# The recurrence's conv of block B ahead of the norm's scaling, that of C among the first four output blocks

## The chip, the cores and the metric

One Trainium2 chip, one core. The metric is the device time of one execution in microseconds (us), as the median of several runs.

## What is computed

One inference step of a small hybrid decoder: one Mamba-2 layer (SSD, a recurrence over chunks of tokens), then one multi-head latent attention layer with a paged cache, for 8 sample sequences of 4 new tokens, 16 meta tokens and a prompt of 256, in all TOK = 304 columns. The change touches the Mamba layer alone:

```python
h = rmsnorm(x, norm_g)
proj = h @ w_in                                  # z | x, B, C | dt
xbc, conv_new = causal_conv(xbc, conv_prev, ...) # 4 taps, bias, then silu
...                                              # the recurrence gives y
y = y * silu(z)
yg = y.reshape(bt, L, 8, 512)                    # 8 groups
yg = yg * rsqrt(mean(yg * yg) + EPS)             # the norm, group by group
return x + (yg * gate_norm) @ w_out
```

The channels fall into 8 groups. A group has four blocks of 128 channels of z, four of x, one of B and one of C; B and C are the fifth and sixth block that the convolution runs over (`xB = 4`, `xC = 5`).

## The kernel before

All work is written out by hand for five engines, with semaphores between them. TensorE multiplies in float32r in three products for every pair (`mm3`, L110 to L112: high by high, low by high, high by low). Weights come in units of 1 MB: SP loads `raw` (L588), ACT makes the high part `w_hi` (`split`, L935, two halves), POOL subtracts it to make the low part `w_lo` (L720, two halves); two buffers of each.

The loop runs over g, the groups. In a turn g:

- TensorE makes the ten input blocks of group g (`in_block`, k = 0 to 9: z 0 to 3, then x 0 to 3, B at k = 8, C at k = 9), with steps of the recurrence of group g - 1 between them (`heads(g - 1, k)`); the last, at k = 8, is the sum of squares of y, `squares`.
- Then it makes the sixteen output blocks of group g - 1 (`out_block`, c = 0 to 15, 12 products each), with steps that prepare group g between them (`start(g, c)`: at c = 6 x is turned, at c = 9 B and C are used). An output block needs `y_lo` (c = 0: half one for its first six products, half two for the rest), its weights, and a free bank: it waits until DVE's work on the block two before is done.

DVE goes through the same order. `evac` takes an input block out of its bank (L1096, L1097) into `cbuf[k % 2]` one iteration later than TensorE made it; `add_out` (L1101) adds an output block to x. `conv(g, k)` runs the taps of a block: tap 0 is L1115, taps 1 to 3 are L1117 on the same accumulator `cacc`, then two small copies keep the last columns (L1122, L1123) and raise `conv_saved`. Each tap waits for the one before (`v`). Tap 0 waits for the evacuation and for `old_done`, which ACT raises when it has put the old columns in front (`conv_past`, L943). The blocks x 0 to 3 have their conv at k = 5 to 8. B's four taps stand at c = 0 to 3, one behind each `add_out`, and C's at c = 4 to 7.

At k = 9 DVE evacuates B, then runs `heads(g - 1, 9)`: `scaled` (L1227, four instructions, y times the norm's factor and gain; waits for `y_rstd`) and `y_low` (L1233, two halves, waits for ACT's `y_hi`, L1006). ACT at k = 9: a split, `conv_past` of B, then `root` (L999, L1001: `y_rstd`) and `y_hi` twice. After that it has, for c < 16, four rounds n: a split, then n = 0: silu of z and `conv_silu` of x 0 to 3; n = 1: `conv_silu` of B and C (L956, L958), which waits for C's conv; n = 2 and 3: `e_cum` and `decay`. SP at n = 1 stores `conv_new` once it is saved and loads `s_t` after `xc_done`.

In turn 0 there is no group before: the input blocks come in another order and no output block is made.

Of the kernel before, what the change touches and what calls it, by code (L numbers as in the profile page):

```python
# [515 lines left out]
def mamba_stage(nc, m, psum, d, stores):  # L516
# [36 lines left out]
    xB, xC = 4, 5  # L553
# [17 lines left out]
    def block_wait(eng, kind, g, k):  # L571
        eng.wait_ge(blk_done, at[kind, g, k] + 1)

    def in_wait(eng, kind, g, k):
        eng.wait_ge(in_out, in_at[kind, g, k] + 1)

    with nc.Block() as block:
# [505 lines left out]
        def _(dve):  # L1083
            v = Serial(dve, dve_step)

            def evac(kind, g, k):
                block_wait(dve, kind, g, k)
                src, rs = DENSE[at[kind, g, k] % 2], m["rs"]
                if kind == "z":
                    if k == 0:  # L1090
                        y_gated.wait(dve, g - 2, PAIRS - 1)
                    nc.vector.tensor_tensor(gate[g % 2][:, k, :], src[:, 0:TOK], rs[:], ALU.mult).then_inc(in_out, 1)
                else:
                    conv_saved.wait(dve, g if k >= 2 else g - 1, k - 2 if k >= 2 else CONV_BLK - 2 + k)
                    buf = cbuf[k % 2]
                    nc.vector.tensor_tensor(by_seq(buf, 7)[:, :, 3:7], by_seq(src, 4), by_seq(rs, 4), ALU.mult)  # L1096
                    nc.vector.tensor_tensor(buf[:, 59:CB], src[:, N_SAMPLE:TOK], rs[:, N_SAMPLE:TOK], ALU.mult).then_inc(in_out, 1)  # L1097
# [5 lines left out]
            def conv(g, k, taps=range(4)):  # L1103
                buf, acc = cbuf[k % 2], cacc[:, k, :]
                cw = lambda t: m["conv_w"][:, g, k, t:t + 1]
                new = conv_new[g % 2]
                for t in taps:
                    if t == 0:
                        in_wait(dve, "c", g, k)
                        old_done.wait(dve, g, k)  # L1110
                        if k == 0:
                            ys_done.wait(dve, g - 1, 1)
                            if g >= 2:
                                dve.wait_ge(conv_stored[g % 2], 16 * (g // 2))
                        v(nc.vector.tensor_scalar(acc, buf[:, 0:CO], cw(0), m["conv_b"][:, g, k:k + 1], ALU.mult, ALU.add))  # L1115
                        continue
                    ins = nc.vector.scalar_tensor_tensor(acc, buf[:, t:t + CO], cw(t), acc, op0=ALU.mult, op1=ALU.add)  # L1117
                    if t < 3:
                        v(ins)
                        continue  # L1120
                    ins.then_inc(conv_done.sem, 1)
                    nc.vector.tensor_copy(new[:, k, 0:DEC_BATCH, :], by_seq(buf, 7)[:, :, 4:7])  # L1122
                    nc.vector.tensor_copy(new[:, k, DEC_BATCH, :], buf[:, CB - 3:CB]).then_inc(conv_saved.sem, 1)  # L1123
# [5 lines left out]
            def x_back(g, n):  # L1129
                t = TILE_ORDER[n]  # L1130
                rows, h = TILE_N[t], slice(g * HPG, (g + 1) * HPG)
                xn_done.wait(dve, g, n)
                y_done.wait(dve, g - 1, PAIRS - 1)
                sp_done.wait(dve, g - 1, 0)
                if g == 0 and n == 0:
                    dve.wait_ge(steps.stored, 16)
                times(m["xdt"][0:rows, t, :], XN[n][0:rows, :], m["dt_n"][0:rows, t, h])
                times(m["xwp"][0:rows, t, :], XN[n][0:rows, :], m["wp_n"][0:rows, t, h]).then_inc(xn_out.sem, 1)

            def samples_back(g):  # L1140
                xn_done.wait(dve, g, 3)
                up_done.wait(dve, g - 1, 3)
                times(m["xws"][:, :], CBA[:, REP], m["ws_q"][:, g, :], 2).then_inc(xn_out.sem, 1)

            def b_back(g):
                bn_done.wait(dve, g, 0)
                nc.vector.tensor_copy(m["b_n"][0:48, 0, :], BN[0:48, 0:STATE]).then_inc(bn_out.sem, 1)
                nc.vector.tensor_copy(m["b_n"][:, 1:3, :], BN[:, STATE:3 * STATE].rearrange("p (t n) -> p t n", t=2)).then_inc(bn_out.sem, 1)

            def b_spread(g):  # L1150
                wide = [P, DEC_BATCH, STATE]
                nc.vector.tensor_tensor(m["b_diag"][:], BN[:, 3 * STATE:4 * STATE].rearrange("p (a n) -> p a n", a=1).to_broadcast(wide),
                                        m["diag"][:].rearrange("p (b a) -> p b a", a=1).to_broadcast(wide), ALU.mult).then_inc(bd_done.sem, 1)

            def c_spread(g):
                xc_done.wait(dve, g, 1)
                nc.vector.tensor_copy(m["c_diag"][:, :, 0:DEC_SEQ], xc[:, xC, 0:N_SAMPLE].rearrange("p (b t) -> p b t", t=DEC_SEQ)).then_inc(cd_done.sem, 1)

            def cb_back(g):
                cb_done.wait(dve, g, 0)  # L1160
                nc.vector.tensor_tensor(m["cb"][0:48, 0:304], CBA[0:48, 0:304], m["mask"][0:48, 0:304], ALU.mult).then_inc(cb_out.sem, 1)
                cb_done.wait(dve, g, 1)
                nc.vector.tensor_tensor(m["cb"][:, 304:688], CBB[:, 0:384], m["mask"][:, 304:688], ALU.mult).then_inc(cb_out.sem, 1)

            def skip(g, p):
                ins = nc.vector.tensor_scalar(y[:, p, :], xc[:, p, :], m["d_skip"][:, g, p:p + 1], None, ALU.mult)
                if p == PAIRS - 1:
                    ins.then_inc(y_set.sem, 1)

            def mix(g, e):  # L1170
                dec_done.wait(dve, g, e)
                cb_out.wait(dve, g, 1)
                dc = dec_at(g, e)
                if g == LAST and e >= 2:
                    nc.vector.tensor_tensor(dc[0:48, 0:304], dc[0:48, 0:304], m["cb"][0:48, 0:304], ALU.mult)
                    nc.vector.tensor_tensor(dc[:, 304:688], dc[:, 304:688], m["cb"][:, 304:688], ALU.mult).then_inc(mix_done.sem, 1)
                else:
                    nc.vector.tensor_tensor(dc[:], dc[:], m["cb"][:], ALU.mult).then_inc(mix_done.sem, 1)
# [88 lines left out]

            def start(g, c):
                if c < 4:
                    conv(g, xB, (c,))  # L1270
                elif c < 8:
                    conv(g, xC, (c - 4,))
                elif c < 11:
                    if c == 8:
                        samples_back(g)
                    x_back(g, c - 8)
                if c == 9:
                    c_spread(g)
                if c == 11:
                    cb_back(g)  # L1280
                if c == 12:
                    b_back(g)
                if c == 13:
                    b_spread(g)
                if c == 14:
                    skip(g, 0)
                    skip(g, 1)
                if c == 15:
                    skip(g, 2)
                    skip(g, 3)  # L1290
                if g == LAST and c >= 14:
                    mix(g, c - 14)
# [31 lines left out]
            for g in range(GROUPS):  # L1324
                of_g = blocks[at["z" if g else "c", g, 0]:][0:IN_UNITS]
                if g == 0:
                    evac(*of_g[0])
                    conv(0, 0)
                    evac(*of_g[1])
                    conv(0, 1)  # L1330
                    steps.rooted(dve)
                    steps.sums(dve)
                    evac(*of_g[2])
                    conv(0, 2)
                    evac(*of_g[3])
                    steps.turned_back(dve)
                    conv(0, 3)
                    evac(*of_g[4])
                for k in range(IN_UNITS if g else 0):
                    if k:  # L1340
                        evac(*of_g[k - 1])
                    elif g == 1:
                        evac("z", 0, PAIRS - 1)
                    heads(g - 1, k)
                    if 5 <= k < 9:
                        conv(g, k - 5)
                for c in range(KT):
                    if g == 0 and c % 4 == 0:
                        evac(*of_g[CONV_BLK - 1 + c // 4])
                    if g and c == 0:  # L1350
                        evac(*of_g[IN_UNITS - 1])
                    if g:
                        add_out(g - 1, c)
                    start(g, c)
# [1743 lines left out]
```

## Time and profile before

| | us |
|---|---|
| median of 3 runs | 2270.61 (2270.43 to 2272.24) |
| the profiled execution | 2272.74 |
| its span, first to last instruction | 2271.0 |
| PE busy | 2172.0 (96% of the span) |
| DVE busy | 1423.9 (63%) |
| ACT busy | 1081.5 (48%) |
| POOL busy | 1063.0 (47%) |

The Mamba layer fills roughly the first 950 us. Times in the trace are counted from the span's start. Busy PE is time in which a matmul is in the array; matmuls overlap, so the distance from one start to the next is what they cost. A time in brackets behind an instruction is the idle time of its engine before it, with what ended it.

### The profile page before, as it was taken

To read this page: it belongs to the slowest core of one execution; us is meant where nothing else is said; L and a number is where in the kernel's file an instruction comes from. 1 tells how busy PE (TensorE), PEld (TensorE's weight loads), DVE (VectorE), ACT (ScalarE), POOL (GpSimd) and SP (SyncE) were. 2 spreads that over 40 slices of the span, in tenths; PEclk is the share of its full clock that TensorE was granted. 3 is DMA by queue.
4 is the path that set the end of the run, shared out by engine and by line. 5 is a ranking of instruction groups with operands and counts; after the bars stand their busy time and mean duration, and the time that the engine had idled before them with its cause. 6 is when DMAs were issued, how large, how long until landed. Compare 5 with 4: busy or idle time off the path is not lost. (4 is left out here: it accounts for less than half of the span.)

```text
span 2271.0 us, 37449 instructions
## 1 busy us (share of the span) xinstructions
PE 2172.0 (96%) x13816; PEld 1864.2 (82%) x13816; DVE 1423.9 (63%) x2329; ACT 1081.5 (48%) x2696; POOL 1063.0 (47%) x694
## 2 busy tenths in 40 slices
PE   7999999999999999799998995999999999999799
PEld 7989988899988899598997763787787877877599
DVE  7877777778786868654214667566565665665510
ACT  5454444444444444554344554554554544545332
POOL 2655656565656565266772004533333333333166
PEclk9999999999999999899999996999999999999899
DMA  5664646464656565334443312202122122021544
GB/s 179 228 222 162 225 175 223 152 226 167 219 173 211 182 218 204 126 114 146 166 167 124 132 69 86 74 22 74 31 64 64 32 64 74 22 74 33 226 159 145
DMA packets 80768, 309.69 MB, mean 136 GB/s; under 512 B 14626, under 2 KB 22178, under 8 KB 55250
## 3 DMA queue, kind: packets, MB, share of 16 engines
q1 hardware_dynamic: 80594, 307.41, 39.5%
q8 instruction: 105, 1.72, 0.3%
q14 instruction: 69, 0.57, 0.1%
HBM read 279.72 MB, written 27.66 MB: 135 GB/s over the span
## 5 line engine op out<-in xcount | busy, mean ns | idle before, releaser
L720 POOL TENSOR_TENSOR w_lo<-raw,w_hi 128x1024 fp32r<-128x1024 f32 x216 | 539.4, 2520 | 396.3 <-ACT w_hi L935 396.3
L110 PE MATMUL bank<-h_hi,w_hi 128*128 128x304 f32 (+1 forms) x1520 | 470.2, 309 | 14.4 <-DVE w_lo L339 10.5
L112 PE MATMUL bank<-h_hi,w_lo 128*128 128x304 f32 (+1 forms) x1520 | 458.3, 302 | 0.0
L111 PE MATMUL bank<-h_lo,w_hi 128*128 128x304 f32 (+1 forms) x1520 | 456.5, 300 | 0.0
L935 ACT ACTIVATE w_hi<-raw 128x1024 fp32r<-128x1024 f32 x216 | 216.6, 1050 | 340.2 <-PE bank L112 333.7
L110 PE MATMUL bank<-b_hi,a_hi 128*128 128x512 f32 x896 | 357.6, 399 | 16.1 <-POOL a_lo L2503 8.4
L111 PE MATMUL bank<-b_lo,a_hi 128*128 128x512 f32 x896 | 350.9, 392 | 0.0
L112 PE MATMUL bank<-b_hi,a_lo 128*128 128x512 f32 x896 | 350.5, 391 | 0.0
L110 PEld LDWEIGHTS bank<-h_hi,w_hi 128*128 128x128 f32 x1520 | 286.4, 188 | 26.2 <-DVE w_lo L339 10.5
L111 PEld LDWEIGHTS bank<-h_lo,w_hi 128*128 128x128 f32 x1520 | 286.9, 189 | 2.3 <-issue 1.7
L112 PEld LDWEIGHTS bank<-h_hi,w_lo 128*128 128x128 f32 x1520 | 286.4, 188 | 0.0
L2554 ACT ACTIVATE two<-two 128x128 f32<-128x128 f32 x512 | 152.2, 299 | 146.5 <-DVE two L2775 142.3
L110 PEld LDWEIGHTS bank<-b_hi,a_hi 128*128 128x128 f32 x896 | 169.3, 189 | 60.6 <-issue 9.6
L2503 POOL TENSOR_TENSOR a_lo<-sum,a_hi 128x256 fp32r<-128x256 f32 x128 | 98.2, 768 | 252.0 <-ACT a_hi L2535 252.0
L1654 POOL TENSOR_TENSOR w_lo<-raw,w_hi 128x1024 fp32r<-128x1024 f32 x68 | 164.6, 2442 | 105.0 <-ACT w_hi L1732 105.0
L112 PEld LDWEIGHTS bank<-b_hi,a_lo 128*128 128x128 f32 x896 | 169.2, 189 | 36.1
L111 PEld LDWEIGHTS bank<-b_lo,a_hi 128*128 128x128 f32 x896 | 169.3, 189 | 33.3
L110 PE MATMUL bank<-y_hi,w_hi 128*128 128x304 f32 x512 | 162.8, 318 | 14.3 <-PEq L2942 8.3
L2775 DVE TENSOR_TENSOR one<-bank,one 128x512 f32<-128x512 f32 x192 | 132.0, 688 | 63.1 <-PE bank L112 60.8
L111 PE MATMUL bank<-y_lo,w_hi 128*128 128x304 f32 x512 | 155.7, 304 | 0.0
L112 PE MATMUL bank<-y_hi,w_lo 128*128 128x304 f32 x512 | 155.2, 303 | 0.0
L1117 DVE SCALAR_TENSOR_TENSOR cacc<-cbuf,conv_w,cacc 128x328 f32<-128x328 f32 x144 | 126.7, 880 | 3.6
(395 smaller groups left out, 4306.1 us busy)
## 6 DMA issues: line engine op xcount, KB each, us to landing
raw<-in_a_units SPq DMA_DIRECT2D x111, 1024.0 KB, 5.0
raw<-in_b_in_units SPq DMA_DIRECT2D x20, 1024.0 KB, 4.7
past<-in_cache SPq DMA_DIRECT2D x64, 288.0 KB, 3.2
pt<-in_cache_t SPq DMA_DIRECT2D x64, 256.0 KB, 2.6
raw<-in_o_units SPq DMA_DIRECT2D x16, 1024.0 KB, 5.0
s_in<-in_state_in SPq DMA_DIRECT2D x31, 512.0 KB, 7.1
out_state_out<-s_in SPq DMA_DIRECT2D x31, 512.0 KB, 6.8
s_t<-in_state_t SPq DMA_DIRECT2D x15, 1024.0 KB, 6.3
```

The source lines that it names most:

```text
L110: nc.tensor.matmul(out, a[0], b[0], start=start, stop=False)
L111: nc.tensor.matmul(out, a[0], b[1], start=False, stop=False)
L112: return nc.tensor.matmul(out, a[1], b[0], start=False, stop=stop)
L720: nc.gpsimd.tensor_tensor(w_lo[u % 2][:, c], raw[u % 2][:, c], w_hi[u % 2][:, c].bitcast(F32), ALU.subtract).then_inc(lo_done, 1)
L935: nc.scalar.activation(w_hi[u % 2][:, c], raw[u % 2][:, c], ACT.Copy).then_inc(hi_done, 1)
L1117: ins = nc.vector.scalar_tensor_tensor(acc, buf[:, t:t + CO], cw(t), acc, op0=ALU.mult, op1=ALU.add)
L1654: nc.gpsimd.tensor_tensor(w_lo[n % 2][:, c], raw[n % 2][:, c], w_hi[n % 2][:, c].bitcast(F32), ALU.subtract).then_inc(lo_done, 1)
L2503: nc.gpsimd.tensor_tensor(m[f"a_lo{n}"][:], operand(q, n), m[f"a_hi{n}"][:].bitcast(F32), ALU.subtract).then_inc(a_lo.sem, 1)
L2554: last = nc.scalar.activation(c, c, ACT.Square, accum_out=ss[u][:, page, 4 * c4 + h:4 * c4 + h + 1])
L2775: nc.vector.tensor_tensor(dst[g][:], bank_of(q, n, g), src[g][:], ALU.add).then_inc(added.sem, 1)
```

## The change

In turns g >= 1, B's conv is taken out of the output blocks and stands whole at k = 9, behind the evacuation of B and ahead of `heads(g - 1, 9)`, with its `scaled` and `y_low`. C's four taps move from c = 4 to 7 up to c = 0 to 3. At c = 4 to 7 only `add_out` stays. Turn 0 is as before. The other engines' programs are untouched.

```diff
             def start(g, c):
                 if c < 4:
-                    conv(g, xB, (c,))
+                    if g == 0:
+                        conv(g, xB, (c,))
+                    else:
+                        conv(g, xC, (c,))
                 elif c < 8:
-                    conv(g, xC, (c - 4,))
+                    if g == 0:
+                        conv(g, xC, (c - 4,))
                 elif c < 11:
                     if c == 8:
                         samples_back(g)
@@
                 for k in range(IN_UNITS if g else 0):
                     if k:
                         evac(*of_g[k - 1])
+                        if k == 9:
+                            conv(g, xB)
                     elif g == 1:
                         evac("z", 0, PAIRS - 1)
                     heads(g - 1, k)
```

## Rows read from the trace of the kernel before

**Rows 1.** Table of windows: length; busy us (count) by engine; PE clock, DMA, GB/s.
```profile
419.40:536.70 117.30, 116.34 (x845) 105.52 (x844) 90.86 (x143) 55.22 (x91) 70.05 (x28) 1.00 0.57 195
654.00:771.30 117.30, 116.34 (x845) 105.52 (x844) 90.85 (x143) 55.21 (x91) 70.06 (x28) 1.00 0.56 195
```

**Rows 2.** List of waits, 302.5 to 888.6 us: total us, times, longest.
```profile
ACT xc L956 <- DVE cacc L1117: 44.8, 5, 9.0
...
PEld bank L110 <- DVE x L1101: 13.7, 25, 0.8
```

**Rows 3.** Timeline of PE, turn g = 3: start, us, instruction; blocks 0, 1, 4, 6.
```profile
419.43 0.30 PE L110 MATMUL bank<-y_hi,w_hi 128*128 128x304 f32 x1
...
421.11 0.31 PE L110 MATMUL bank<-y_hi,w_hi 128*128 128x304 f32 x1
...
426.62 0.41 PE L110 MATMUL bank<-y_hi,w_hi 128*128 128x304 f32 x1 [0.31 <-DVE x L1101]
...
430.80 0.41 PE L110 MATMUL bank<-y_hi,w_hi 128*128 128x304 f32 x1 [0.56 <-DVE x L1101]
```

**Rows 4.** Timeline of DVE around the norm's scaling, turn g = 3.
```profile
411.02 0.43 DVE L1097 TENSOR_TENSOR cbuf<-bank,rs 128x272 f32<-128x272 f32 x1
...
414.01 0.82 DVE L1227 SCALAR_TENSOR_TENSOR y<-y,gate_norm,y_rstd 128x304 f32<-128x304 f32 x1 [2.56 <-ACT y_rstd L1001]
...
414.76 2.66 DVE L1227 SCALAR_TENSOR_TENSOR y<-y,gate_norm,y_rstd 128x304 f32<-128x304 f32 x1
...
417.33 0.97 DVE L1227 SCALAR_TENSOR_TENSOR y<-y,gate_norm,y_rstd 128x304 f32<-128x304 f32 x2
...
418.23 1.65 DVE L1233 TENSOR_TENSOR y_lo<-y,y_hi 128x608 fp32r<-128x608 f32 x2
...
421.31 0.47 DVE L1101 TENSOR_TENSOR x<-x,bank 128x304 f32<-128x304 f32 x1 [0.98 <-PE bank L112]
```

**Rows 5.** Timeline of ACT, the same stretch.
```profile
412.88 0.21 ACT L943 ACTIVATE cbuf<-conv_old 128x24 f32<-128x24 f32 x1
...
418.34 0.71 ACT L1006 ACTIVATE y_hi<-y 128x608 fp32r<-128x608 f32 x1 [0.18 <-DVE y L1227]
...
419.69 1.06 ACT L935 ACTIVATE w_hi<-raw 128x1024 fp32r<-128x1024 f32 x1 [0.64 <-PE bank L112]
```

**Rows 6.** Timeline of POOL, one in turn 0, the others in turn 3.
```profile
87.28 2.41 POOL L720 TENSOR_TENSOR w_lo<-raw,w_hi 128x1024 fp32r<-128x1024 f32 x1
...
412.11 2.40 POOL L720 TENSOR_TENSOR w_lo<-raw,w_hi 128x1024 fp32r<-128x1024 f32 x1 [3.37 <-ACT w_hi L935]
...
414.46 2.62 POOL L720 TENSOR_TENSOR w_lo<-raw,w_hi 128x1024 fp32r<-128x1024 f32 x1
...
420.83 2.41 POOL L720 TENSOR_TENSOR w_lo<-raw,w_hi 128x1024 fp32r<-128x1024 f32 x1 [3.75 <-ACT w_hi L935]
...
423.20 2.50 POOL L720 TENSOR_TENSOR w_lo<-raw,w_hi 128x1024 fp32r<-128x1024 f32 x1
...
427.54 2.71 POOL L720 TENSOR_TENSOR w_lo<-raw,w_hi 128x1024 fp32r<-128x1024 f32 x1 [1.84 <-ACT w_hi L935]
...
430.22 2.39 POOL L720 TENSOR_TENSOR w_lo<-raw,w_hi 128x1024 fp32r<-128x1024 f32 x1
```

**Rows 7.** Timeline of DVE among the output blocks 0 to 4, turn 3.
```profile
421.69 1.74 DVE L1115 TENSOR_SCALAR cacc<-cbuf,conv_w,conv_b 128x328 f32<-128x328 f32 x1
...
423.86 2.20 DVE L1117 SCALAR_TENSOR_TENSOR cacc<-cbuf,conv_w,cacc 128x328 f32<-128x328 f32 x1
...
427.93 2.37 DVE L1122 COPY conv_new<-cbuf 128x24 f32<-128x24 f32 x1
430.22 0.16 DVE L1123 COPY conv_new<-cbuf 128x3 f32<-128x3 f32 x1
```

**Rows 8.** Timeline of DVE, taps of an x block with POOL idle.
```profile
400.88 1.75 DVE L1117 SCALAR_TENSOR_TENSOR cacc<-cbuf,conv_w,cacc 128x328 f32<-128x328 f32 x3
```

**Rows 9.** Timeline of DVE, turn 0, beside POOL's instruction of 87.28.
```profile
87.30 2.43 DVE L1157 COPY c_diag<-xc 128x32 f32<-128x32 f32 x1
```

## The prediction

> **What bounds the kernel now.** Only the recurrence's group loop is edited, so I read that stretch. First the table of windows over two periods, each from the first output block of one turn to that of the next: both last 117.30 us, and PE is busy 116.34 us in each, at full granted clock [rows 1]. TensorE sets the pace, and the turns repeat. Then the list of waits over the five turns g = 2 to 6: TensorE's weight loads wait for DVE's `add_out` (L1101) for 13.7 us in all [rows 2]; it is the one entry of that list in which TensorE waits for another engine. What it costs in time is read from the matmul starts. In turn g = 3 the first output block starts at 419.43, the next at 421.11, so a block takes 1.68. The fifth starts at 426.62, 7.19 after the first where 4 x 1.68 = 6.72 would do: 0.47 lost. The seventh starts at 430.80, 4.18 later where 3.36 would do: 0.82 lost [rows 3]. A turn has 1.29 us that the edit can win. Why these two exist: a block waits for the `add_out` of two blocks before, and that stood behind a conv step that took 2.20 (L1117) and 2.37 us (L1122) [rows 7] where three L1117 alone take 1.75 [rows 8].
>
> **The rule behind the long steps.** POOL's subtractions (L720) run at 420.83 to 423.24, 423.20 to 425.70, 427.54 to 430.25 [rows 6]. L1115 ends at 423.43, 0.19 behind the first; L1117 at 426.06, 0.36 behind the second; L1122 at 430.30, 0.05 behind the third [rows 7]. So a DVE instruction that has all its operands in SBUF and starts inside a POOL subtraction ends with it; `scaled` (L1227) shows the same, 2.66 us for 0.5 [rows 4]. `add_out`, with a bank operand, takes 0.47 always. Who is first holds: L1123 started with POOL's instruction at 430.22 and took 0.16, L1157 started 0.02 behind one, at 87.30, and took 2.43 [rows 6, 7, 9].
>
> The Trainium skill (SBUF — State Buffer, Who interferes with whom) says that VectorE instructions with two SBUF inputs, and one-input copies in the 2-port mode, share a port pair with GpSimd, and that the first to issue blocks the other entirely. The trace agrees (2.20, 2.37, 2.66 us), and the rule speaks against placing B's conv here: by it the median is 2275.2 or more, without it the 2261.6 of the second rival.
>
> **Part 1: B's conv ahead of `scaled`, seven times (g = 1 to 7).** DVE is through with the evacuation at 411.45 and then idle 2.56 us until `y_rstd` at 414.01 [rows 4]. Unhindered, conv costs some 0.4 + 1.75 + 0.2 = 2.4 us (three L1117 [rows 8]; L1115 estimated from `add_out`'s 0.47 at nearly its width, the copies from L1123's 0.16, overlapped), so it looks as if it fits. It does not. Tap 0 waits for `old_done`, given by ACT's L943, which ends at 413.09 [rows 5]. 1.64 of the idle 2.56 us is unusable. At 413.12 POOL's subtraction of 412.11 to 414.51 is under way [rows 6]. Tap 0 ends 0.19 behind it, at 414.69. Tap 1 is inside the second subtraction, which started at 414.46. With a tap 0 let in ahead such a second one takes 2.50 (as at 423.20), so ends at 416.96. Tap 1 ends 0.36 later, 417.32. Taps 2 and 3 free: 0.59 each (1.75/3), end 418.50. Two copies overlap the tail, and `scaled` can start at 418.57.
>
> Four free L1227 take 3 x 0.45 + 0.52 = 1.88 (two of them cover 417.33 to 418.30 [rows 4]): end E = 420.45. Before, E was 418.30. But before, the same E led to `y_lo` half one 418.23 to 419.01, earliest PE start 419.06, and PE arrived only at 419.43 as its block of C had just ended. That 0.37 slack is used up. New start of the first output block: E + 0.76 = 421.21, 1.78 late by these rows (each rounded to 0.01; I take 1.74, which leaves 0.04 for their overlaps). A matmul restarted after a wait delays its follower by 0.11 (estimate: 0.41 against 0.30 long [rows 3]). **Cost 1.85 us a turn.** The second half of `y_lo` and the evacuation of C follow within 1.3 us of that start, before PE wants them.
>
> **Part 2: C in output blocks 0 to 3, nothing in 4 to 7.** Call the new first start Y. ACT's split (L935) started at 419.69 after waiting 0.64 for PE [rows 5]; now it directly follows `y_hi`, at Y - 0.11. POOL starts 1.14 behind it (419.69 to 420.83): subtractions at Y+1.03 to 3.44 and 3.40 to 5.90. C's tap 0 (queued behind `add_out` 0 at Y+1.99) ends Y+3.63; tap 1 ends Y+6.26; `add_out` 2 runs Y+6.29 to 6.76, PE sees it at 6.81 and wants it at 6.82. The fifth block's gap of 0.47 is gone, but for about 0.10 of restart, as the wait is met only just. Taps 2 and 3 follow by Y+8.20, with `add_out` 3 between.
>
> Now the copies. L1122 starts at Y+8.12, L1123 at Y+8.20. The next subtraction follows PE's fourth block, not DVE: 427.54 was 8.11 behind 419.43, with 0.11 of restart it is Y+8.22. Both copies start before it, by 0.10 and by 0.02. By "first holds" they pass (430.22 passed level with POOL), `add_out` 4 is on time and the 0.82 is won. **Gain 0.47 - 0.10 + 0.82 = 1.19 us a turn.**
>
> **Edits at nothing.** `conv_silu` of B and C on ACT stood 9.0 us waiting for C (44.8 in five turns [rows 2]); that goes. Queued behind it are a split, `e_cum` and two decays; they come 2 us or more earlier, no PE wait in rows 2 is for them. What is late next is PE itself. On SP the store of `conv_new` and the load of `s_t` wait for these same steps and go out some 8 us earlier, between two weight loads. The cover is that the next split waits for PE anyway (0.64 idle [rows 5]); if a weight load were held up 1 us beyond its cover it would cost 1 us a turn. POOL's next subtraction comes earlier too and may catch `c_spread`; a hit costs up to 2.43 [rows 9] on DVE, where the wait for the next block covers it. Group 0's turn is unchanged by its branch. In g = 1 the norm starts later for table loads, with conv blocked by the same two subtractions; I take the same 1.85.
>
> **Sum.** 1.85 - 1.19 = 0.66 us, times 7 = +4.6 us. The profiled execution took 2272.74 us (span 2271.0 and 1.7 around it), 2.1 over the median 2270.61. So 2277.3 for such an execution, and a median of **2275.2 us**.
>
> **Rivals.** First, the copies are caught (0.30). The margin of 0.02 us comes from a dozen added steps. If L1123 falls behind POOL's start, it ends with it: 8.22 + 2.4 = Y+10.6, `add_out` 4 ends 11.07, the seventh block starts Y+11.12 instead of 10.2 to 10.3. Relative to 430.80 - 419.43 = 11.37 only 0.25 is won of both gaps: net 1.74 - 0.25 = 1.49 a turn, +10.4 in seven, 2281.0 us. For it: L1157's 2.43 at a lag of 0.02. Against: the level start at 430.22.
>
> Second, on the other side, the taps slip past POOL (0.07). It decides at the border of the two subtractions at 414.46: if DVE gets tap 1 in as well as tap 0, tap 2 is the one that waits, `scaled` starts 0.59 earlier, the cost is 1.26 and the net +0.07, 2271 us; if no tap waited, conv would end at 413.12 + 2.4 = 415.5 and four free L1227 at 417.5, ahead of 418.30, so that nothing is paid and 1.29 x 7 = 9.0 won: 2261.6. Against: at this very border `scaled` got one instruction in (0.82) and the next took 2.66 [rows 4].
>
> Third, more is lost (0.08): a weight load or split held up: over 12 us, 2283 and up.
>
> The Trainium skill's rule (same section) gives the pair to whoever issues first; by it L1123 passes, 2275.2; were POOL served first, 2281.0. No row has a lag of -0.02.
>
> **Chances and range.** Forecast 0.55, rivals 0.30, 0.07, 0.08. The forecast's own range is 2273.5 to 2277; with the second case the range is 2272.5 to 2283.0, and leaves about 0.18 out. What a measurement here can tell from no change is 0.2%, 4.5 us, and +4.6 lies on that line: of the 0.55, 0.28 goes to same and 0.27 to slower. The slipping case gives 0.05 to faster and 0.02 to same. Faster 0.05, same 0.28 + 0.02 = 0.30, slower 0.27 + 0.30 + 0.08 = 0.65.
>
> **What would show it.** Turns of about 117.9 us (forecast) or 118.8 (copies caught). In a turn: L1115 of B long (about 1.6), one L1117 of about 2.6, four L1227 of 0.53 each, a PE wait for `y_lo` (DVE L1233) of 1.7 to 1.8 ahead of the first output block. Then L1122 of C at 0.17 and no wait for `add_out` over 0.2, or L1122 or L1123 over 2.3 and one PE wait of 0.9. Wrong if L1227 is still stretched, if the PE wait for `y_lo` is absent, or if the turns differ from each other.

## The result and the profile after

The changed kernel takes 2275.26 us in the median of 20 runs (2272.98 to 2278.22), the kernel before 2270.66 (2268.92 to 2274.56, 20 runs). The ratio is 1.0017, with a 95% interval of 1.0011 to 1.0024: 2.5 to 5.5 us slower, 4.6 in the medians. The predicted time was 2275.2. The slowdown is clear of no change, but at 0.17% it is a little smaller than the 0.2% that the prediction held to be just measurable.

The table of windows of the changed kernel, for two periods from first output block to first output block (columns as in [rows 1]):

```profile
422.04:539.86 117.82, 116.05 (x844) 105.51 (x844) 87.90 (x143) 55.09 (x92) 69.59 (x28) 1.00 0.56 193
657.70:775.52 117.82, 116.05 (x843) 105.52 (x844) 87.88 (x143) 55.09 (x92) 69.58 (x28) 1.00 0.55 194
```

A turn is 117.82 to 117.84 us instead of 117.30: 0.53 us more, seven turns. PE's busy time is all but the same (116.05 for 116.34), so it is idle time that grew. DVE is even 3 us less busy, as fewer of its steps are held up by POOL. The list of waits of 302.5 to 888.6 us says where (total us, times, longest):

```profile
DVE cacc L1115 <- ACT cbuf L943: 8.7, 5, 1.8
PE bank L110 <- DVE y_lo L1233: 8.4, 5, 1.7
...
PEld bank L110 <- DVE x L1101: 5.9, 10, 0.8
```

The list of the kernel before also had an entry of the matmuls themselves, 0.31 and 0.56 us in each turn, the two gaps of [rows 3]:

```profile
PE bank L110 <- DVE x L1101: 4.4, 10, 0.6
```

Two entries are new: tap 0 of B waits 1.75 us for ACT's L943 in each of the five turns, and TensorE waits 1.67 us for `y_lo` in each. No matmul waits for `add_out` any more. The wait of the weight loads for it is down from 13.7 in 25 places [rows 2] to 5.9 in 10, and in turn g = 3 these leave no gap between the products. Also the 44.8 us of `conv_silu` waiting for C are gone. The timeline of DVE in turn g = 3:

```profile
411.79 0.43 DVE L1097 TENSOR_TENSOR cbuf<-bank,rs 128x272 f32<-128x272 f32 x1
413.96 1.49 DVE L1115 TENSOR_SCALAR cacc<-cbuf,conv_w,conv_b 128x328 f32<-128x328 f32 x1 [1.75 <-ACT cbuf L943]
415.49 3.77 DVE L1117 SCALAR_TENSOR_TENSOR cacc<-cbuf,conv_w,cacc 128x328 f32<-128x328 f32 x3
419.17 0.17 DVE L1122 COPY conv_new<-cbuf 128x24 f32<-128x24 f32 x1
419.25 0.16 DVE L1123 COPY conv_new<-cbuf 128x3 f32<-128x3 f32 x1
419.32 1.87 DVE L1227 SCALAR_TENSOR_TENSOR y<-y,gate_norm,y_rstd 128x304 f32<-128x304 f32 x4
421.10 1.65 DVE L1233 TENSOR_TENSOR y_lo<-y,y_hi 128x608 fp32r<-128x608 f32 x2
...
424.38 1.16 DVE L1115 TENSOR_SCALAR cacc<-cbuf,conv_w,conv_b 128x328 f32<-128x328 f32 x1
...
426.13 2.04 DVE L1117 SCALAR_TENSOR_TENSOR cacc<-cbuf,conv_w,cacc 128x328 f32<-128x328 f32 x1
...
430.05 0.17 DVE L1122 COPY conv_new<-cbuf 128x24 f32<-128x24 f32 x1
430.13 0.16 DVE L1123 COPY conv_new<-cbuf 128x3 f32<-128x3 f32 x1
```

and of POOL and PE beside it:

```profile
412.87 2.39 POOL L720 TENSOR_TENSOR w_lo<-raw,w_hi 128x1024 fp32r<-128x1024 f32 x1 [3.37 <-ACT w_hi L935]
...
415.22 2.48 POOL L720 TENSOR_TENSOR w_lo<-raw,w_hi 128x1024 fp32r<-128x1024 f32 x1
...
422.95 2.40 POOL L720 TENSOR_TENSOR w_lo<-raw,w_hi 128x1024 fp32r<-128x1024 f32 x1 [5.25 <-ACT w_hi L935]
...
430.23 2.42 POOL L720 TENSOR_TENSOR w_lo<-raw,w_hi 128x1024 fp32r<-128x1024 f32 x1 [2.42 <-ACT w_hi L935]
```
```profile
420.06 0.30 PE L112 MATMUL bank<-h_hi,w_lo 128*128 128x304 f32 x1
422.04 0.38 PE L110 MATMUL bank<-y_hi,w_hi 128*128 128x304 f32 x1 [1.67 <-DVE y_lo L1233]
```

B's conv runs from 413.96 to 419.4, 5.4 us, where the same six instructions take 2.4 unhindered. Its first tap ends at 415.45, 0.19 behind POOL's first subtraction; the second, inside the three of 415.49, at 418.06, 0.36 behind POOL's second. Scaling, no longer hindered itself, starts at 419.32, 4.6 us after `y_rstd` was ready (414.75), and the first output block starts 1.98 us after the last product of the input blocks (start to start). In the kernel before it was 0.13, so the start is 1.85 late:

```profile
419.30 0.30 PE L112 MATMUL bank<-h_hi,w_lo 128*128 128x304 f32 x1
419.43 0.30 PE L110 MATMUL bank<-y_hi,w_hi 128*128 128x304 f32 x1
```

Among the output blocks C's conv stands where B's stood, but both PE gaps of [rows 3] are gone: the copies at 430.05 and 430.13 are through before POOL starts at 430.23.

The two profiled executions differ less than the medians: their spans are 2271.0 and 2271.2. The first output block of g = 7 is 4.7 us later than before (893.34 for 888.63). Its last `add_out` is 3.4 later (926.95 for 923.53), as the gaps of that turn are gone too, but the scaling behind it only 1.1 (948.87 for 947.77), and the end of the Mamba layer 0.6. From 929.55 on (932.98 after) DVE runs the same steps with nearly the same lengths; TensorE's sum of squares (L865) differs, running mostly at the lower granted clock (1.2 GHz) before and at the full one after. TensorE's L865 starts every 0.51 us before and every 0.27 us after, and DVE's scaling follows it. Where the stretches at 1.2 GHz lie differs between these two executions, so the medians, and within one trace the equal turns, are what is compared here.

### The profile page after: what moved, and what is told of

Same layout as the page of the kernel before. It is cut to its first block and busy times, and to the rows that moved or that the text cites. A ratio compares the mean times of both kernels' runs of the same rounds, so it can differ in the third digit from the quotient of the medians.

```text
span 2271.2 us, 37428 instructions
## 1 busy us (share of the span) xinstructions
PE 2168.5 (95%) x13816; PEld 1861.5 (82%) x13816; DVE 1404.5 (62%) x2329; ACT 1081.0 (48%) x2696; POOL 1059.3 (47%) x694
## 5 line engine op out<-in xcount | busy, mean ns | idle before, releaser
L1117 DVE SCALAR_TENSOR_TENSOR cacc<-cbuf,conv_w,cacc 128x328 f32<-128x328 f32 x144 | 137.5, 955 | 4.4
```

## Experiments

In all of them the result is told by the time and by the length of a turn, first output block to first output block, which repeats to 0.02 us where nothing else is said. Each was timed beside the kernel before on the same chip. The times of the cut copy are of 4 runs, those of two experiments of the last part of 2 each, the others of 5 to 11. Edits add lines, so L1232 or L1106 of an experiment are `scaled` and `add_out` here.

### Part 1 alone

```diff
 # changed kernel, start(g, c)
                 if c < 4:
                     if g == 0:
                         conv(g, xB, (c,))
-                    else:
-                        conv(g, xC, (c,))
                 elif c < 8:
-                    if g == 0:
-                        conv(g, xC, (c - 4,))
+                    conv(g, xC, (c - 4,))
```

> The changed kernel with C's four taps left at output blocks 4 to 7, so only part 1 (B's conv ahead of scaling) is done. Theory (TensorE is lost only at the start of output block 0, and both gaps of before go because nothing of conv stands at blocks 0 to 3; C's place is worth nothing): turn of 117.8 us as in the changed kernel (117.84), PE wait for y_lo 1.7, time within 2 us of the changed kernel, about 2275. Rival (the earlier C, with conv_silu and the s_t load ahead, is what pays for the delay): the turn is 0.5 to 1.2 us longer, 118.3 to 119.0, and the time 2278 to 2283.

Measured: 2274.69 us (2272.61 to 2276.01) beside 2269.99 of the kernel before, ratio 1.0019 (1.0009 to 1.0028); turn 117.83; the wait for `y_lo` 1.67:

```profile
421.37 0.38 PE L110 MATMUL bank<-y_hi,w_hi 128*128 128x304 f32 x1 [1.67 <-DVE y_lo L1233]
```

So the earlier C, with `conv_silu` and the load of `s_t` ahead, moves the turn by no more than 0.01 us. The gain of the change is that B's conv no longer stands at output blocks 0 to 3 (C's, there instead, costs nothing in the changed kernel); the loss is the late start of block 0.

### The margin of the copies

```diff
 # changed kernel, conv(g, k, taps)
-    nc.vector.tensor_copy(new[:, k, 0:DEC_BATCH, :], by_seq(buf, 7)[:, :, 4:7])
+    parts = 4 if g and k == xC else 1
+    for i in range(parts):
+        b = slice(i * DEC_BATCH // parts, (i + 1) * DEC_BATCH // parts)
+        nc.vector.tensor_copy(new[:, k, b, :], by_seq(buf, 7)[:, b, 4:7])
```

> The changed kernel with C's first copy (L1122) cut into four pieces of two sequences each, same data; the last copies start some 0.24 us later, behind the start of POOL's subtraction at Y+8.19 instead of 0.10 ahead of it. Theory (who starts first holds the port): a copy is caught and takes about 2.4 us, add_out 4 comes 2 us late, one PE wait of 0.8 to 1.0 us ahead of the seventh output block, turn 118.7 to 118.9, time about 2282. Rival (small copies pass a running subtraction, or the margin doesn't matter): turn 117.8, time about 2275.

Measured: 2284.54 us, ratio 1.0060 (1.0045 to 1.0075); turn 118.91. DVE's timeline, POOL's and PE's in turn g = 3:

```profile
433.36 2.62 DVE L1125 COPY conv_new<-cbuf 128x6 f32<-128x6 f32 x4
435.90 0.15 DVE L1126 COPY conv_new<-cbuf 128x3 f32<-128x3 f32 x1
```
```profile
433.54 2.42 POOL L720 TENSOR_TENSOR w_lo<-raw,w_hi 128x1024 fp32r<-128x1024 f32 x1 [2.40 <-ACT w_hi L935]
```
```profile
436.48 0.42 PE L110 MATMUL bank<-y_hi,w_hi 128*128 128x304 f32 x1 [0.81 <-DVE x L1101]
```

The same 24 columns cost 1.08 us a turn when cut in four: three pieces pass, the fourth starts 0.04 us behind POOL's start at 433.54 and takes 2.41 us, to POOL's end. The time rose by 14.5 us over the kernel before, and seven turns of 1.61 make 11.3; the interval of the ratio (10.2 to 17.0 us) holds both.

### `old_done` early, POOL as it is

```diff
 # changed kernel, ACT's loop over k
                 for k in range(first_in):
+                    if g and k == 9:
+                        conv_past(*of_g[k - 1])
                     split(u + k + 1)
...
-                    if k:
+                    if k and not (g and k == 9):
                         conv_past(*of_g[k - 1])
```

> The changed kernel with ACT's conv_past of B ahead of its split at k = 9, so that old_done is raised long before DVE wants it; POOL as before. Theory (wait for old_done costs 1.7 us of the idle window, but POOL's two subtractions then hinder two of the later taps): tap 0 and tap 1 free at 411.5 to 412.5 (turn g = 3 in the clock of before), taps 2 and 3 held to the ends of the two subtractions, scaling starts 0.7 earlier, turn 117.1, time about 2270. Rival A (the wait alone is the cause): conv over before y_rstd, no PE wait for y_lo, turn 116.0 to 116.2, about 2263. Rival B (POOL alone is the cause): nothing changes, turn 117.8.

Measured: 2270.10 us, ratio 0.9998 (0.9989 to 1.0007); turn 117.11. DVE and POOL, turn g = 3:

```profile
411.74 0.45 DVE L1117 TENSOR_SCALAR cacc<-cbuf,conv_w,conv_b 128x328 f32<-128x328 f32 x1
412.22 5.79 DVE L1119 SCALAR_TENSOR_TENSOR cacc<-cbuf,conv_w,cacc 128x328 f32<-128x328 f32 x3
```
```profile
412.36 2.68 POOL L720 TENSOR_TENSOR w_lo<-raw,w_hi 128x1024 fp32r<-128x1024 f32 x1 [3.37 <-ACT w_hi L935]
...
415.00 2.65 POOL L720 TENSOR_TENSOR w_lo<-raw,w_hi 128x1024 fp32r<-128x1024 f32 x1
```

With `old_done` out of the way tap 0 runs at once, but the three taps behind it take 5.79 us instead of 1.75: the first is free, and each of the other two ends 0.36 behind one of the subtractions. The wait for `y_lo` shrinks to 0.95. Neither rival holds: neither the wait nor POOL is the cause alone.

### Both out of the way

```diff
 # the edits of the experiments above (ACT's early conv_past, C at blocks 4 to 7), and on POOL:
+            gated_by = {unit_at(g) + IN_UNITS: g - 1 for g in range(1, GROUPS)}
             for u in range(2, LAST_UNIT + 2):
+                if u in gated_by:
+                    yn_done.wait(pool, gated_by[u], 1)
                 for n, c in enumerate(HALVES):
```

> The changed kernel with three edits: conv_past of B ahead of ACT's split at k = 9; POOL's subtraction for the first output unit waits until scaled is done (yn_done of both halves); C's taps back at output blocks 4 to 7. Theory (both the wait for old_done and POOL's two subtractions make B's conv late, and the gaps among the output blocks go when blocks 0 to 3 are free of conv): L1115 and L1117 of B at 0.44 and 0.56, scaling starts with y_rstd as in the kernel before, low half one of the weights ready 0.5 us ahead of TensorE, no PE wait for y_lo nor for add_out, turn 116.0, time 2261 to 2263. Rival (POOL's held work now makes TensorE wait for weights, or y_lo's second half is caught by it): a PE wait for w_lo or y_lo of 0.5 to 2 us, turn 116.5 to 118, time 2265 to 2275.

Measured: 2263.58 us (2262.12 to 2264.63), ratio 0.9970 (0.9958 to 0.9982); turn 115.90. DVE and POOL, turn g = 3, and the window of a turn:

```profile
411.07 0.45 DVE L1120 TENSOR_SCALAR cacc<-cbuf,conv_w,conv_b 128x328 f32<-128x328 f32 x1
411.55 1.75 DVE L1122 SCALAR_TENSOR_TENSOR cacc<-cbuf,conv_w,cacc 128x328 f32<-128x328 f32 x3
...
413.58 1.88 DVE L1232 SCALAR_TENSOR_TENSOR y<-y,gate_norm,y_rstd 128x304 f32<-128x304 f32 x4
415.38 3.68 DVE L1238 TENSOR_TENSOR y_lo<-y,y_hi 128x608 fp32r<-128x608 f32 x2
```
```profile
415.54 5.79 POOL L723 TENSOR_TENSOR w_lo<-raw,w_hi 128x1024 fp32r<-128x1024 f32 x2 [7.23 <-DVE y L1232]
```
```profile
419.01:534.91 115.90, 115.81 (x845) 105.50 (x844) 87.57 (x143) 55.31 (x91) 70.45 (x29) 1.00 0.57 197
```

This is the theory read backwards. B's conv fits the idle 2.5 us, scaling starts as long before the first output block as it did in the kernel before (5.4 us), and of 115.90 us PE is idle 0.09. The hold-up by POOL has only moved: now the second half of `y_lo` is caught (3.68 us for two of 0.79), where it still has time. The only flaw was turn 1, with its table loads ahead of `y_rstd`:

```profile
187.14 0.38 PE L110 MATMUL bank<-y_hi,w_hi 128*128 128x304 f32 x1 [1.91 <-issue]
```

There POOL is held until 184.2, and the first half of its subtractions ends at 187.04, 0.10 before the block starts. So TensorE waits for the weights there, though the profile calls it "issue".

### The same without its flaw: the fastest

`for g in range(2, GROUPS)` in the line of `gated_by`.

> As e5_gate_c_late, but POOL is held from turn g = 2 on. In turn 1 two table loads put y_rstd 1.3 to 2.3 us later than elsewhere, and with the hold TensorE waited 1.9 us for weights there. Theory (that wait goes, a smaller one for y_lo of 0.4 to 0.8 stays): turns of 115.9 as in e5, the first output block of turn 1 1.3 to 1.7 us earlier, time 1 to 2 us under e5's 2263.6. Rival (that wait is covered by the gap it would leave elsewhere): same time as e5.

Measured: 2261.72 us (2260.79 to 2264.48) beside 2271.56 of the kernel before, ratio 0.9959 (0.9945 to 0.9972); turns of 115.90, and the first output block of turn 1 at 185.05 instead of 187.14. It beats both kernels, the changed one by about 13.5 (not on the same chip). It is 1.9 us under the run with the hold in turn 1 too, but the two were not timed on the same chip. The block of turn 1 came 2.1 us earlier, where 1.3 to 1.7 had been expected; its remaining wait for `y_lo` is 0.95.

### Which of the three edits does it

POOL held and C at blocks 4 to 7, but `conv_past` of B left behind ACT's split:

> As e5_gate_c_late, but with conv_past of B left behind ACT's split, so tap 0 waits for old_done. Theory (that wait costs 1.6 us of the idle window even with POOL out of the way; scaling ends at 417.5 in the clock of the kernel before, and POOL's held subtraction starts only then): PE waits 0.9 to 1.3 for the weights' low part ahead of the first output block, turn 117.0 to 117.4. Rival (POOL alone was the cause, old_done costs nothing): turn 115.9.

Measured: 2271.58 us, ratio 0.9997 (0.9987 to 1.0007); turns of 116.99. PE's wait is no longer for `y_lo` but for the weights' low part: POOL starts it only at 418.82, and its first half ends at 421.69, 0.09 before PE goes on. The profile calls this wait "issue":

```profile
421.78 0.38 PE L110 MATMUL bank<-y_hi,w_hi 128*128 128x304 f32 x1 [0.83 <-issue]
```
```profile
418.82 5.78 POOL L723 TENSOR_TENSOR w_lo<-raw,w_hi 128x1024 fp32r<-128x1024 f32 x2 [8.73 <-DVE y L1230]
```

POOL held and `conv_past` early, but C at blocks 0 to 3 as in the change:

> As e5_gate_c_late, but C's four taps at output blocks 0 to 3 as in the changed kernel. Theory (the gaps among the output blocks come from any conv at blocks 0 to 3 once the first output block is on time, as POOL's subtractions then lie over it as in the kernel before): B's conv free, no PE wait for y_lo, but PE waits for add_out ahead of the fifth or seventh block of 1.0 to 1.4 in sum, turn 117.0 to 117.4. Rival (the gaps had to do with B's place only): turn 115.9 as in e5.

Measured: 2291.57 us (2 runs; ratio 1.0087, 1.0069 to 1.0106); turns of 117.33 to 121.80, no longer equal. Two of them in the table of windows:

```profile
544.53:661.86 117.33, 116.35 (x845) 105.54 (x844) 88.51 (x143) 55.31 (x91) 70.50 (x29) 1.00 0.56 195
783.56:905.36 121.80, 118.23 (x845) 107.02 (x844) 92.53 (x143) 55.40 (x91) 70.64 (x29) 0.99 0.53 187
```

And in a long turn of 120.16:

```profile
313.19 2.61 DVE L1122 SCALAR_TENSOR_TENSOR cacc<-cbuf,conv_w,cacc 128x328 f32<-128x328 f32 x1
315.72 2.32 DVE L1127 COPY conv_new<-cbuf 128x24 f32<-128x24 f32 x1
```
```profile
300.83 10.60 POOL L723 TENSOR_TENSOR w_lo<-raw,w_hi 128x1024 fp32r<-128x1024 f32 x4 [7.22 <-DVE y L1232]
313.04 4.97 POOL L723 TENSOR_TENSOR w_lo<-raw,w_hi 128x1024 fp32r<-128x1024 f32 x2 [1.61 <-ACT w_hi L938]
```
```profile
318.54 0.41 PE L110 MATMUL bank<-y_hi,w_hi 128*128 128x304 f32 x1 [2.55 <-DVE x L1106]
```

The direction was right, the size was not: I had one step caught per subtraction pair, and at some alignments the last tap and the copy behind it are caught one after the other, which makes PE wait 2.55 us at one block. POOL's next pair starts at 313.04, 0.15 ahead of the tap at 313.19, and holds it and the copy behind it. In the changed kernel the last copy is 0.10 us ahead of POOL; what being behind costs there is seen only for one copy (118.91).

The kernel before with POOL held and nothing else:

> The kernel before with one edit: POOL's subtraction for the first output unit waits until scaled is done. Theory (scaling had 0.4 us of slack, so freeing it gains nothing; B's conv stays at blocks 0 to 3 with its gaps): L1227 at 0.53 each, turn 117.0 to 117.5. Rival (holding POOL back is by itself what made e5 faster): turn 116.0 to 116.5.

Measured: 2292.20 us (2 runs; ratio 1.0090, 1.0072 to 1.0109); turns of 117.35 to 121.80, by the same pair of caught steps, here B's. Four runs of `scaled` at 0.53 gained nothing, as it had slack, and holding POOL by itself is harmful. The fast version needs the early `conv_past` (without it 116.99 a turn) and C at blocks 4 to 7 (without it 117.3 to 121.8). That it needs the hold is shown only with C at blocks 0 to 3 (117.11 without it); the early `conv_past` with C at blocks 4 to 7 and POOL free was not run.

## Why the prediction was right, point by point

**The cost of part 1** was put at 1.85 us a turn: the start of the first output block 1.74 late, and 0.11 for the product behind it. Measured, the start is 1.85 late (1.98 against 0.13) and the second product comes 0.21 behind the first where 0.14 is usual, 0.07 more: 1.92. The run with both causes out of the way gives the same: 117.83 less 115.90 is 1.93. Each step held: tap 0 kept until 0.19 behind the first subtraction, tap 1 until 0.36 behind the second, four free L1227. Taking away one cause gave back 0.72 (early `conv_past`) or 0.84 (held POOL), both 1.93. The start was mis-sized because I had TensorE start 0.05 behind `y_lo`; it took 0.15 (421.89 to 422.04).

**The gain of part 2** was put at 1.19 and is 1.40: it is the 117.30 of the kernel before less the 115.90 without both gaps and without the late start. Two terms were mis-sized. The gaps of 0.47 and 0.82 leave out the delay behind the seventh block's own restart, 0.11 (0.41 against 0.30 long [rows 3]). And the 0.10 kept for a restart at the fifth block was not needed. As TensorE started later behind `y_lo`, POOL's subtractions lay 0.12 earlier against the blocks (Y+0.91 for the forecast Y+1.03), tap 1 ended sooner and the fifth block met no wait. With it the last copy passed by 0.10 us and not by 0.02. One reading was wrong too, without weight in the sum: the wait of the weight loads was not the only one in which TensorE waits for another engine, as the list has the matmuls' own 4.4 us, for the same `add_out`.

**The sum.** Cost and gain were both put too low, by 0.08 and 0.21, which partly cancels: net 0.53 a turn for the forecast 0.66. Seven turns make 3.7 us (3.4 in the traces up to the last `add_out`), the forecast had 4.6. The medians differ by 4.6, the ratio makes it 3.9, with an interval of 2.5 to 5.5. That the forecast meets the median to hundredths is luck; 0.9 us of the difference of the medians is not shown by the turns, and what it is stays open within that interval.

**The rivals.** That the copies are caught did not happen, but is real: the cut copy made it happen, with 118.91 us a turn where 118.8 had been worked out for it. That the taps slip past POOL did not happen. What it would win if they did was put at 9.0 us. With POOL held, `old_done` early and C left at blocks 4 to 7, 9.8 us were measured (interval 6.4 to 12.5; 7 x 1.40 = 9.8). With C at blocks 0 to 3, where the change has it, the same two edits lost 20 us. As holding POOL does harm there by itself, no run shows whether this rival's win would have come in the changed kernel as it stands. The edits put at nothing were that: the earlier C, `conv_silu` and `s_t` moved the turn by no more than 0.01 us.

## What to carry to other kernels

Idle time of an engine is a place to move work to only after two questions are answered for that very window: when the moved step's own inputs are ready, and what runs meanwhile on an engine that can hold the step up, here POOL. Here 2.56 idle us seemed to hold 2.4 us of work; the input came 1.75 us late, and POOL more than doubled the rest (5.4 us). Once the moved step is on the path, the remedy can be on a third engine: 0.2 us of ACT's work put earlier and POOL's work held back 3.9 us (idle 7.23 before it for 3.37), with C left where it was, turned a loss of 0.2% into a gain of 0.4%. And such a hold has to be looked at over the whole turn: alone, in the kernel before, it lost 0.9%.

## What the runs showed of the hardware

The border of two subtractions decides by hundredths. DVE copies of 3 columns that started 0.10 us ahead of POOL's instruction took 0.16 us; of the four pieces begun from 433.36 on, against a POOL start at 433.54, the one begun 0.04 ahead passed and the one 0.04 behind was held to its end, and so small a copy then costs 2.4 us. I had not expected that POOL pays too: with a tap running at its start (0.42 us of it left) its instruction is 2.68 us long instead of 2.40, and with `y_lo` (0.79 us) running, two take 5.79. The same hold-ups make equal turns unequal: in the run with C at blocks 0 to 3 and POOL held, turns of 117.3 and 121.8 us stand in one execution.

The Trainium skill (SBUF — State Buffer, Who interferes with whom) has the first to issue hold the port for its whole instruction. The rows above agree in both directions, down to copies of 3 to 24 columns.
